# TensorE runs gate and up of the next expert ahead of the down products of this one; the lead buffers hold four experts

## The reference

```python
def grouped_experts(xf, expert, gate, w_gate, w_up, w_down):
    ...
    def run_block(args):
        xb, e = args
        return (jax.nn.silu(xb @ w_gate[e]) * (xb @ w_up[e])) @ w_down[e]
    yb = lax.map(run_block, (buf.reshape(n_blk, ROW_BLOCK, d), blk_expert))
    y = yb.reshape(rows, d) * row_w[:, None].astype(xf.dtype)
    return jax.ops.segment_sum(y, row_tok, num_segments=t)
```

## Time and profile before

| | |
|---|---|
| median of 3 runs | 1672.23 us (1670.7 to 1678.46) |
| the profiled execution's own time | 1673.83 us |
| its span in the trace | 1672.0 us |
| PE busy | 1380.5 us (83%) |
| DVE, ACT, POOL busy | 383.6, 341.1, 218.8 us |
| mean TensorE clock granted | 0.935 |
| DMA: moved, mean over the span | 472.58 MB, 283 GB/s |
| experts of layer 0, first gate_up to last down | 276.7 to 754.9 us |
| experts of layer 1, first gate_up to last down | 1161.3 to 1640.6 us |

### The profile page before, as it was taken

How to read it: one execution, slowest core, us unless ns; L and a number is a source line. 1 busy time by engine, 2 the same in 40 slices (tenths; PEclk the granted TensorE clock), 3 DMA queues, 4 the chain that set the end, 5 groups by cost and what they waited for, 6 DMA issues and landing times. The chain is left out here.

```text
span 1672.0 us, 17836 instructions
## 1 busy us (share of the span) xinstructions
PE 1380.5 (83%) x6689; PEld 766.2 (46%) x6689; DVE 383.6 (23%) x721; ACT 341.1 (20%) x657; POOL 218.8 (13%) x380
## 2 busy tenths in 40 slices
PE   5999994998888887786999877895998878888882
PEld 4999772332322222234667755774333223222220
DVE  3434423000000000005422477623000000000003
ACT  5213320000000000004534354421100000000002
POOL 2000000221111111111000132101111111111111
PEclk9999996999999999997999989996999999999996
DMA  9020426999999999985122200306999999999984
GB/s 344 33 102 1 176 107 281 423 383 424 427 427 426 425 426 427 425 350 208 51 74 78 101 1 1 152 38 271 407 377 426 427 426 426 425 426 425 424 377 158
DMA packets 60341, 472.58 MB, mean 283 GB/s; under 512 B 10528, under 2 KB 10604, under 8 KB 35712
## 3 DMA queue, kind: packets, MB, share of 16 engines
q1 hardware_dynamic: 45904, 441.48, 63.7%
q0 software_dynamic: 14384, 30.36, 4.9%
HBM read 465.17 MB, written 23.13 MB: 292 GB/s over the span
## 5 line engine op out<-in xcount | busy, mean ns | idle before, releaser
L927 PE MATMUL ps<-ring,act 128*64 128x512 f32 x1920 | 476.8, 650 | 84.5 <-DMA ring<-in_e_up 78.8
L927 PEld LDWEIGHTS ps<-ring,act 128*64 128x64 f32 x1920 | 149.9, 142 | 406.5 <-issue 406.5
L894 PE MATMUL ps<-parts 128*128 128x512 f32 (+1 forms) x1104 | 269.2, 403 | 7.2 <-DVE parts L1193 6.6
L948 PE MATMUL ps<-ring,act 128*64 128x512 f32 x960 | 219.2, 597 | 33.2 <-ACT act L742 33.2
L1376 DVE TENSOR_TENSOR act<-act,ps 128x256 f32<-128x256 f32 x64 | 26.9, 421 | 883.9 <-ACT act L740 883.9
L894 PEld LDWEIGHTS ps<-parts 128*128 128x128 f32 (+1 forms) x1104 | 196.0, 179 | 70.2 <-issue 7.7
L880 PE MATMUL ps<-parts 128*128 128x264 f32 x1152 | 143.9, 287 | 4.5 <-DVE parts L1188 2.9
L880 PEld LDWEIGHTS ps<-parts 128*128 128x128 f32 x1152 | 142.6, 190 | 5.5 <-issue 5.5
L740 ACT ACTIVATE act<-ps 128x256 f32<-128x256 f32 x64 | 24.5, 383 | 587.6 <-PE ps L927 587.6
L948 PEld LDWEIGHTS ps<-ring,act 128*64 128x64 f32 x960 | 75.8, 136 | 135.2 <-issue 135.2
L1188 DVE TENSOR_TENSOR parts<-ring,parts 128x1024 fp32r<-128x1024 f32 x64 | 77.8, 1225 | 117.9 <-ACT parts L673 117.7
(11 more groups left out here) (164 smaller groups left out, 897.9 us busy)
## 6 DMA issues: line engine op xcount, KB each, us to landing
ring<-in_e_gate SPq DMA_DIRECT2D x60, 2048.0 KB, 17.1
ring<-in_e_up SPq DMA_DIRECT2D x60, 2048.0 KB, 21.6
ring<-in_e_down SPq DMA_DIRECT2D x60, 2048.0 KB, 21.7
ring<-in_a_w_in SPq DMA_DIRECT2D x6, 2048.0 KB, 20.5
arena<-in_e_up SPq DMA_DIRECT2D x4, 2048.0 KB, 12.5
arena<-in_e_gate SPq DMA_DIRECT2D x4, 2048.0 KB, 7.6
arena<-in_e_down SPq DMA_DIRECT2D x4, 2048.0 KB, 12.5
ring<-in_w_kv SPq DMA_DIRECT2D x4, 2048.0 KB, 14.0
```

The source lines that it names most:

```text
L894: last = mm(bank, x[:, k, :], w[:, k, :], start=(k == 0 and i == 0), stop=(k == KC - 1 and i == 2))
L927: last = mm(ps[f * C:(f + 1) * C, 2 + b, :].rearrange("p (g m i) -> p g m i", g=2, i=2), x, w, start=(k == 0), stop=(k == KC - 1))
L948: last = mm(ps[o * C:(o + 1) * C, 6 + b, :], hT[:, b, (2 * c + a) * C:(2 * c + a + 1) * C], w[:, f * D + o * DH:f * D + (o + 1) * DH], sta ...
```

## The change

It does four things.

1. PE computes gate_up(n+1) ahead of the second part of expert n. Its order becomes gate_up(n+1), turn_block(n+2), turn_hidden(n), down(n). To start, it turns both first blocks: turn_block(0), gate_up(0), turn_block(1), and then the loop. DVE's `take_x` follows: it takes the same half that it has just freed (expert n+2 behind hidden n).
2. The lead buffers hold experts 0, 3, 6 and 9 (`LEAD`); five pairs (`EARLY`) are written out, and the loops start at pair 5. The ring serves the other 28.
3. The waits for weights go by experts: `gate_up_done` and `down_done` count experts, and `unit_used` is brought up to date once at the end of a layer.
4. Expert 3's gate and up are loaded as halves; the first two halves go out when half of gate_up(0) is done (`lead_half_used`).

POOL's program is not changed, nor is any arithmetic. The diff, cut to its core:

```diff
@@ expert_unit
-            if early:
-                n = U_MOE[layer] + 3 * (2 * q + u - 1) + ORDER.index(part)
-                return n % RING, landing(n)
-            n = U_MOE[layer] + 3 * u + ORDER.index(part)
-            return n % RING, landing(n) - 16 + 16 * q
+            n = U_MOE[layer] + 3 * ring_turn(2 * (q if early else EARLY) + u) + ORDER.index(part)
+            return n % RING, landing(n) + (0 if early else 16 * (q - EARLY))
@@ SP, experts
+                def load_lead(ex):
+                    uses = E * layer + LEAD[LEAD.index(ex) - 1] + 1
+                    if ex == LEAD[1]:
+                        for a in range(2):
+                            if a == 0:
+                                sp.wait_ge(lead_half_used, layer + 1)
+                            else:
+                                sp.wait_ge(gate_up_done, uses)
+                            for b, part in enumerate(("gate", "up")):
+                                expert_load(layer, part, bass.ds(ex, 1), lead_w[:, b, :], lead_landed, slice(a * UNIT // 2, (a + 1) * UNIT // 2))
+                    else:
+                        sp.wait_ge(gate_up_done, uses)
+                        for b, part in enumerate(("gate", "up")):
+                            expert_load(layer, part, bass.ds(ex, 1), lead_w[:, b, :], lead_landed)
+                    sp.wait_ge(down_done, uses)
+                    expert_load(layer, "down", bass.ds(ex, 1), lead_down, lead_down_landed)
                 def pair(q):
                     for u in range(2):
                         for part in ORDER:
-                            load(q * 2 + 2 + u, u, part, q * 6 + (U_MOE[layer] - 6 + 3 * u + done[part]))
+                            load(q * 2 + u, u, part, q * 2 + (E * layer + u - 1))
...
+                for ex in range(3, 2 * EARLY):
+                    if ex in LEAD:
+                        load_lead(ex)
+                    else:
+                        for part in ORDER:
+                            load(ex, ring_turn(ex) % 2, part, E * layer + IN_RING[ring_turn(ex) - 2] + 1)
+                with sp.Fori(EARLY, PAIRS) as q:
                     pair(q)
@@ PE, moe
-                pe.wait_ge(gathered[layer][0], 16)
-                turn_block(0).then_inc(x_turned, 1)
-                pair(0, True, False)
-                pair(1, True, False)
-                with pe.Fori(2, PAIRS - 1) as q:
-                    pair(q, False, False)
-                pair(PAIRS - 1, False, True)
+                def pair(q, early):
+                    for u in range(2):
+                        if u == 0:
+                            products(q, 1, early)
+                        else:
+                            products(q + 1, 0, early and q + 1 < EARLY)
+                        pe.wait_ge(gathered[layer][u], q * 16 + 32)
+                        turn_block(u).then_inc(x_turned, 1)
+                        finish(q, u, early)
+                for u in range(2):
+                    pe.wait_ge(gathered[layer][u], 16)
+                    turn_block(u).then_inc(x_turned, 1)
+                    if u == 0:
+                        products(0, 0, True)
+                for q in range(EARLY):
+                    pair(q, True)
+                with pe.Fori(EARLY, PAIRS - 1) as q:
+                    pair(q, False)
+                finish(PAIRS - 1, 0, False)
+                products(PAIRS - 1, 1, False)
+                finish(PAIRS - 1, 1, False)
+                pe.wait_ge(down_done, E * (layer + 1))
+                pe.sem_inc(unit_used, 3 * (E - len(LEAD)))
@@ DVE, pair
-                        if not (last and u == 1):
-                            dve.wait_ge(x_turned, E * layer + q * 2 + u + 2)
-                            take_x(1 - u).then_inc(xT_ready, 1)
+                        if not last:
+                            dve.wait_ge(x_turned, q * 2 + (E * layer + u + 3))
+                            take_x(u).then_inc(xT_ready, 1)
```

More of the change, by code:

```diff
@@ L49 @@
 RING = 6
+LEAD = (0, 3, 6, 9)
+EARLY = 5
 UNIT = KC * W
+IN_RING = [e for e in range(E) if e not in LEAD]
 U_IN, U_AOUT = 0, 6
 U_MOE0 = U_AOUT + 4
-U_KVQ = U_MOE0 + 3 * (E - 2)
+U_KVQ = U_MOE0 + 3 * (E - len(LEAD))
 U_QT = U_KVQ + 12
@@ L435, in experts, with load @@
             def experts(layer):
-                done = {"gate": 2, "up": 2, "down": 3}
-                def load(ex, u, part, wait):
+                done = {"gate": gate_up_done, "up": gate_up_done, "down": down_done}
+                def load(ex, u, part, uses):
                     n = U_MOE[layer] + 3 * u + ORDER.index(part)
-                    sp.wait_ge(unit_used, free_at[n % RING] if wait is None else wait)
+                    if uses is None:
+                        sp.wait_ge(*free_at[n % RING])
+                    else:
+                        sp.wait_ge(done[part], uses)
@@ L731, in moe, with pair @@
                         nc.scalar.activation(lam[:, 2:4], lam[:, 0:2], ACT.Exp).then_inc(lam_exp, 1)
-                def pair(q, early):
+                def pair(q, first):
                     for u in range(2):
[L735 to L739, removed]
+                        act.wait_ge(gate_up_done, q * 2 + (E * layer + u + 1))
                         nc.scalar.activation(silu[:, u, :], ps[:, 2 + u, 0:FE // 2], ACT.Silu).then_inc(silu_ready, 1)
@@ L742, in pair @@
                         nc.scalar.copy(hT[:, u, :], ps[:, 4 + u, 0:FE // 2]).then_inc(hT_ready, 1)
[L743 to L746, removed]
+                        act.wait_ge(down_done, q * 2 + (E * layer + u + 1))
                         if not first:
@@ L917, in logits, with gate_up @@
                 last.then_inc(logits_done, 1)
-            def gate_up(b, pair_w):
+            def gate_up(b, pair_w, halfway=None):
                 for k in range(KC):
@@ L992, in moe @@
                 table_rows(0, nt).then_inc(tabled, 1)
-                def pair(q, early, last_pair):
-                    for u in range(2):
[L996 to L1001, removed]
-                        else:
[L1003 to L1023, removed]
@@ L1025, in moe, with products @@
-                pe.wait_ge(gathered[layer][0], 16)
-                turn_block(0).then_inc(x_turned, 1)
-                pair(0, True, False)
-                pair(1, True, False)
-                with pe.Fori(2, PAIRS - 1) as q:
-                    pair(q, False, False)
-                pair(PAIRS - 1, False, True)
+                def products(q, u, early):
+                    if early and 2 * q + u in LEAD:
+                        pe.wait_ge(lead_landed, lead_landing(layer, 2 * q + u))
+                        w = lead_w
+                    else:
+                        (gs, gv), (us, uv) = (expert_unit(layer, q, u, part, early) for part in ("gate", "up"))
+                        pe.wait_ge(ring_landed[gs], gv)
+                        pe.wait_ge(ring_landed[us], uv)
+                        w = ring[:, gs:us + 1, :]
+                    pe.wait_ge(xT_ready, q * 2 + (E * layer + u + 1))
+                    gate_up(u, w, lead_half_used if early and q == u == 0 else None).then_inc(gate_up_done, 1)
@@ new lines, in finish @@
+                def finish(q, u, early):
+                    pe.wait_ge(hidden_ready, q * 2 + (E * layer + u + 1))
+                    turn_hidden(u).then_inc(hidden_turned, 1)
+                    if early and 2 * q + u in LEAD:
+                        pe.wait_ge(lead_down_landed, 16 * (len(LEAD) * layer + LEAD.index(2 * q + u) + 1))
+                        w = lead_down
+                    else:
+                        ds, dv = expert_unit(layer, q, u, "down", early)
+                        pe.wait_ge(ring_landed[ds], dv)
+                        w = ring[:, ds, :]
+                    if not (early and q == 0):
+                        pe.wait_ge(y_ready, q * 2 + (E * layer + u - 1))
+                    pe.wait_ge(hT_ready, q * 2 + (E * layer + u + 1))
+                    down(u, w).then_inc(down_done, 1)
```

41 lines of the change are left out of this document (19 added, 22 removed).

## The result

The changed kernel takes 1968.92 us in the median of 4 runs (1966.25 to 1975.29), against 1672.24 us: 1.1775 times as long, with a 95% interval of 1.1743 to 1.1807. Forecast were 1952 us and a range of 1842 to 2021.

What follows compares the result with a forecast made beforehand. Weight loads bound the kernel before, at 15.55 us an expert; after the change the gather would, at 19.9 us, adding 140.7 us in layer 0 and 139.4 in layer 1: 1672.2 + 280 = 1952 us, range 1842 to 2021.

Steps and rivals of the forecast that it cites:

- F(n): The end of down(n) on PE; forecast to come every 18.3 us, or 19.9 us with the slower clock.
- end of down to the gather's issue: From down(n)'s end through ACT's copy and POOL's scatter to the issue of gather n+3: 3.9 us.
- issue to turn_block's start: The gather's landing beside three loads, before turn_block(n+3) can run: 8.9 us, with ends of 8.4 and 9.4.
- turn_block to the end of down at full clock: PE's turn_block 0.75, turn_hidden and the copy 1.03, and down 3.65, behind the gather: 5.43 us.
- added by the clock: PE's steps behind the wait for the gather slow as the granted clock falls: 1.6 us, ends nothing and 2.5.
- that counting costless: The change's counting of semaphores, in the waits for weights, was said to cost nothing that could be found.
- The loads' batch: Down(n+2), then gate and up of n+3, issued by SP at down(n)'s end: landed 18.2 us later, just in time.
- (a): At each layer's start, the first halves of the lead loads go out sooner: 3.7 us gained a layer.
- (b): The transfer dip where PE uses the lead buffers for expert 3 goes, with experts 6 and 9 there: 4.7 us a layer.
- The clock that stays up: Rival: the gather binds the loop but the clock stays at 2.4 GHz, 18.3 us an expert: 1859 us; chance 0.11.
- the hidden gather: Rival: the gather lands within 6.2 us and does not slow the loop, so the change is faster: 1655 us; chance 0.07.
- The rival of SP's shallow queue: Rival: the gather is hidden but SP has fewer loads ahead, 16.3 us an expert: 1690 us; chance 0.03.

Runs made afterwards that it cites:

- experiment 1: The changed kernel with POOL issuing gather n+3 ahead of scatter n and of its wait for y_ready(n): 1715.11 us, 1.0245 times the kernel before.
- experiment 4: The changed kernel with gather n+3 still waiting for y_ready(n) but issued ahead of scatter n, 2.06 us earlier: 1788.42 us.
- experiment 7: The changed kernel with only experts 0 and 3 in the lead buffers and three pairs written out: 1965.21 us.
- experiment 8: The changed kernel with ring loads from the third on in each layer cut to an eighth of their matrix, run for time alone: 1571.18 us in one run.
- experiment 5: The changed kernel with PE and DVE in the order of the kernel before; four lead experts, halves and counting by expert kept: 1661.91 us, 0.9932 of the kernel before.
- Experiment 6: The kernel before's PE and DVE order, only experts 0 and 3 as leads, early halves and counting by expert kept: 1673.52 us, 0.9997 of the kernel before.
- experiment 3: The changed kernel with the gather ahead of the scatter, loads in order of use, and PE's last three steps so ordered: 1664.25 us, 0.9947 of the kernel before.

## Why the prediction was right

**The mechanism** was the forecast one: F(n), `y_ready(n)`, scatter n, gather n+3, turn_block(n+3), F(n+1). 58 waits were forecast; PE waited 58 times, two of them before the first experts, so 56 in the loop. Experiments 1, 4 and 7 show it from three sides, and experiment 8 shows why the gather in it is slow. The terms:

| term, us a turn | forecast | measured at 572 to 593 us |
|---|---|---|
| end of down to the gather's issue | 3.9 | 4.1 |
| issue to turn_block's start | 8.9 | 9.6 |
| turn_block to the end of down at full clock | 5.4 | 5.2 |
| added by the clock | 1.6 | 1.8 |
| sum | 19.9 | 20.7 |

The last two measured rows divide 6.97 us, from turn_block's start at 586.20 to down's end at 593.17. At full clock the same stretch takes 5.19 us in the change, from 294.09 to 299.28, because turn_hidden starts before turn_block has ended; the forecast's 5.43 put one behind the other. So this term was 0.2 too large and the clock's 0.2 too small. The forecast's terms also add up to 19.83, not 19.9, which is 4 us over the 58 loops.

**The landing was sized a little too low** (8.9 and nothing for the wake-up; 9.3 in the median, and PE started 9.6 behind the issue). **A place was missed that paid it back.** The mean of the 29 turns of layer 0 is 20.02 us, (879.92 - 299.28)/29, not 20.7, because two turns in each layer are short; the other 27 average 20.5. That 20.02 lies so near the forecast's 19.9 is luck in part: the two errors go opposite ways. From PE's timeline, and the landing of the gather issued at 440.39:

```profile
431.31 0.72 PE L954 MATMUL ps<-const,nat 128*128 128x128 f32 x4 [1.63 <-DMA nat<-hn_rows,src_now]
...
443.62 0.75 PE L954 MATMUL ps<-const,nat 128*128 128x128 f32 x4
...
462.82 1.10 PE L954 MATMUL ps<-const,nat 128*128 128x128 f32 x4 [6.80 <-DMA nat<-hn_rows,src_now]
```

```profile
nat<-hn_rows,src_now POOLq DMA_INDIRECT x1, 3.1
```

The loop at expert 10 waits for expert 8's products though its buffers are free after expert 7. At the end of down(6) SP issues one load (422.51), the next two only at 429.87 and 430.31, and at the end of down(7) none. The gather of the first short turn is issued at 426.57 beside the one load and lands in 4.6 us; that of the second, at 440.39, meets only the last of the two, which are through by 442.8, and causes no wait at all. In experiment 7, whose loop starts at expert 6, the short turns are those of experts 3 and 4 (13.7 and 13.4 us). I had called that counting costless; with this loop it was even a gain. In layer 1 the mean is 20.24. At the end of a layer down(30) ends 6.2 us behind F(29), not the forecast's 4.7, because PE waits 1.51 us for hidden. Together the expert stretches are 623.4 and 629.1 us where the forecast had 618.9 and 618.7, 15 of the 17 us between 1952 and 1969.

**The loads' batch** was forecast at 18.2 us. The page of the change has medians of 8.2, 12.7 and 17.1 us for down, gate and up of the ring, issued one behind the other. Up is issued 1.0 us behind the end of down (573.47 against 572.48), so the batch is there 18.1 us behind it. It kept up, as forecast: no idle time of gate_up that a load ended is listed.

**The gains (a) and (b)** were rightly counted as gone. On their own they were oversized: 16.8 us forecast, 11.7 measured in experiment 5. Experiment 6 shows that (a), the early halves, is nothing by itself, where the forecast had 7.4 us; (b) alone was not run.

**The rivals.** The clock that stays up (1859) and the hidden gather (1655) did not occur. The rival of SP's shallow queue was no alternative to the forecast but stood behind it: it showed when the gather was taken away, at 41 us above the kernel before (1715.1 against 1673.6) instead of 18. Its working of 16.3 us an expert was too low (16.6 from the end of down(9) to that of down(29), layer 0), and its 17 us of gains were too large (experiment 5). The gate_ups waited by turns, 5.7 to 6.2 us and then not at all in the stretch shown. Bandwidth fell to 318 GB/s in the window of 560 to 580 us (330 forecast), the granted clock's mean fell, and down had its long forms, as forecast.

What the new order is worth with both hindrances removed is experiment 3 against experiment 5: 0.9947 (0.9930 to 0.9964) and 0.9932 (0.9913 to 0.9950) of the kernel before. It gains nothing measurable over the old order; both run at 421 to 428 GB/s in most of their expert slices.

## What to carry to other kernels

When one engine's order is pipelined a step deeper, go through every other engine's program and ask which of its steps now waits for something that comes later: here POOL's gather stood behind a scatter and SP's gate and up behind a down, and neither order had been touched. Price such a wait at the latency under the load that will be beside it, 9 us and not 3. And look first at what bounds the loop: where it moves 426 GB/s already, a better order on TensorE can win only at the start and the end, and here the end became longer.

## What the runs showed of the hardware that was not expected

- Work put into a wait can move the fall of the clock instead of preventing it: with 2.84 us of transposes in the wait turn_block took 0.72 us in most turns, but down then took 5.35; with 5.24 us of them down stayed at 3.65 in 57 of 64 turns.
- A transpose of the same constant block took 0.118 us (2.84 us for 24), while turn_block's four, of `nat`, take 0.75 us, 0.19 each. The runs do not show why.
